# Moving columns of 256 read in turns from the two token blocks, with the weight ring at multiples of 64 bytes

## The reference

```python
z = einsum("bsd,dn->bsn", rmsnorm(x, g_mix), w_in)            # 1024 x 4608
# gated convolution branches, then
x = x + (g_a * (a @ w_a_out) + g_b * (s @ w_b_out)) @ w_o     # 512 x 1024 twice, 1024 x 1024
u = rmsnorm(x, g_ffn) @ w_up                                  # 1024 x 5632
x = x + (gelu(causal_conv(u_gate)) * u_value) @ w_down        # 2816 x 1024
x = x + sigmoid(rmsnorm(x) @ w_ple_gate) * (p @ w_ple)        # 1024 x 1024, 256 x 1024
# second block
proj = rms_norm(x) @ w_in_2                                   # 1024 x 2304, then two attentions
x = x + rms_norm(mix @ w_out_2)                               # 1024 x 1024
c = causal_conv(rms_norm(x) @ w_up_2)                         # 1024 x 8192
x = x + rms_norm((gelu(gate) * value) @ w_down_2)             # 4096 x 1024
```

## Time and profile before

| | us |
|---|---|
| median of 3 runs | 752.45 (752.36 to 752.64) |
| the profiled execution | 752.84 |
| its span, first to last instruction | 750.8 |
| TensorE matmul busy | 743.0 (99%) |
| VectorE busy | 578.7 (77%) |
| ScalarE busy | 452.0 (60%) |
| GpSimd busy | 210.6 (28%) |

### The profile page before, as it was taken

One profiled execution on the slowest core, in us unless ns is written; L12 is line 12 of the kernel. 1 busy time (PEld: TensorE's weight loads), 2 busy tenths in 40 slices (PEclk: granted clock), 3 DMA queues, 4 the chain that ended last, 5 costly groups with the idle time before them and its releaser, 6 DMA issues.

```text
span 750.8 us, 16764 instructions
## 1 busy us (share of the span) xinstructions
PE 743.0 (99%) x5950; PEld 722.7 (96%) x5950; DVE 578.7 (77%) x1049; ACT 452.0 (60%) x765; POOL 210.6 (28%) x136
## 2 busy tenths in 40 slices
PE   9999999999999999999999999999999999999997
PEld 9999999999999999999999999999999999988885
DVE  6899986877887887434987794799999999973333
ACT  7645456556665665445765798876766666643431
POOL 0477642460000000343464003322112212212220
PEclk9999999999999999999999999999999999999999
DMA  8566553565555567544444344365555555666551
GB/s 307 182 217 205 184 166 127 197 201 195 194 180 189 190 204 250 198 162 152 159 161 139 115 134 125 111 199 200 192 190 195 180 184 196 210 212 193 186 179 56
DMA packets 37917, 135.48 MB, mean 180 GB/s; under 512 B 4464, under 2 KB 4720, under 8 KB 37872
## 3 DMA queue, kind: packets, MB, share of 16 engines
q1 hardware_dynamic: 37728, 134.86, 54.4%
q10 hardware_dynamic: 144, 0.00, 0.0%
HBM read 133.80 MB, written 1.05 MB: 180 GB/s over the span
## 4 chain that ended last, share of the span: by engine, by line
PE 89%; DVE 3%; ACT 3%; issue 2%; POOL 1%; DMA 1%; SPq 0%; DVEq 0%; POOLq 0%; ACTq 0%
PE bank L1901 25%; PE bank L1902 25%; PE bank L1903 25%; PE bank L2349 4%; PE bank L2348 4%; PE bank L2347 4%; DVE w_lo L1223 1%; ACT w_hi L787 1%; DMA raw<-in_w_in 1%; POOL X L755 1%; PE bank L2176 1%; ACT score L1079 0%; PE bank L2200 0%; PE bank L1959 0%; DVE sumsq L1813 0%
## 5 line engine op out<-in xcount | busy, mean ns | idle before, releaser
L1901 PE MATMUL bank<-h_hi,w_hi 128*128 128x256 f32 x1372 | 385.9, 281 | 0.3 <-DVE w_lo L1223 0.2
L1902 PE MATMUL bank<-h_lo,w_hi 128*128 128x256 f32 x1372 | 382.9, 279 | 0.0
L1903 PE MATMUL bank<-h_hi,w_lo 128*128 128x256 f32 x1372 | 382.8, 279 | 0.0
L787 ACT ACTIVATE w_hi<-raw 128x1024 fp32r<-128x1024 f32 (+2 forms) x243 | 258.9, 1068 | 93.2 <-PE bank L1903 41.3
L1223 DVE TENSOR_TENSOR w_lo<-raw,w_hi 128x1024 fp32r<-128x1024 f32 (+2 forms) x187 | 236.6, 1268 | 85.9 <-ACT w_hi L787 84.0
L1901 PEld LDWEIGHTS bank<-h_hi,w_hi 128*128 128x128 f32 x1372 | 257.9, 188 | 1.8 <-DVE w_lo L1223 0.7
L1902 PEld LDWEIGHTS bank<-h_lo,w_hi 128*128 128x128 f32 x1372 | 258.0, 188 | 0.0
L1903 PEld LDWEIGHTS bank<-h_hi,w_lo 128*128 128x128 f32 x1372 | 257.9, 188 | 0.0
L636 POOL TENSOR_TENSOR w_lo<-raw,w_hi 128x1024 fp32r<-128x1024 f32 (+1 forms) x56 | 139.0, 2485 | 382.9 <-ACT w_hi L787 374.7
L1281 DVE TENSOR_TENSOR bank<-bank,scales 128x256 f32<-128x256 f32 x116 | 49.5, 430 | 26.3 <-PE bank L1903 17.6
L1572 DVE SCALAR_TENSOR_TENSOR cg<-bank,vec,cg 128x255 f32<-128x255 f32 x108 | 51.5, 476 | 0.7 <-ACT cg L1019 0.6
(11 more groups left out here) (235 smaller groups left out, 963.2 us busy)
## 6 DMA issues: line engine op xcount, KB each, us to landing
raw<-in_w_up SPq DMA_DIRECT2D x108, 512.0 KB, 3.3
raw<-in_w_in SPq DMA_DIRECT2D x53, 512.0 KB, 3.4
raw<-in_w_down SPq DMA_DIRECT2D x32, 512.0 KB, 4.2
raw<-in_w_down SPq DMA_DIRECT2D x16, 704.0 KB, 4.2
raw<-in_w_o SPq DMA_DIRECT2D x8, 512.0 KB, 4.3
raw<-in_w_gate SPq DMA_DIRECT2D x8, 512.0 KB, 3.4
raw<-in_w_out SPq DMA_DIRECT2D x8, 512.0 KB, 3.3
raw<-in_w_b_out SPq DMA_DIRECT2D x4, 512.0 KB, 3.6
```

Of the source, the lines that this page charges most:

```text
L787: nc.scalar.activation(hi_of(u)[:, cols], raw[s][:, cols], ACT.Copy).then_inc(hi_ready, 1)
L1901: nc.tensor.matmul(ps, wh, hi[:, k, :], start=start and n == 0, stop=False)
L1902: nc.tensor.matmul(ps, wh, lo[:, k, :], start=False, stop=False)
L1903: last = nc.tensor.matmul(ps, wl, hi[:, k, :], start=False, stop=stop and n == len(ks) - 1)
```

## The change

The moving columns and the PSUM columns of each 256-column product are put in another order: `in_turns` makes of the 256 columns the sequence tokens 0 to 3, 128 to 131, 4 to 7, 132 to 135, and so on. It is applied to the moving operand and to the output alike, so each token's sum lands in its old place. The access pattern of both operands gets three dimensions, of 32, 2 and 4 elements, with steps of 16, 512 and 4 bytes. The stationary operand, its weight load, the number of instructions, all waits and all DMAs stay.

`RING_PAST` becomes 0. The ring buffers then start 64 bytes past a multiple of 128, from byte 20,416 on, as the activations do. They end where they ended, so X and all that follows keep their addresses. `first_col` becomes 0 everywhere, so that the weights of "down2" from its fourth unit on keep their addresses as well. The first three units of "down2" move by 32 bytes.

```diff
-RING_PAST = 32
+RING_PAST = 0
...
+            def in_turns(columns):
+
+                return columns.rearrange("p (b i e) -> p i b e", b=2, e=4)
+
             def products(ps, s, block0, ks, hi, lo, start, stop, ready=None, w=None):
 
+                ps = in_turns(ps)
                 w_of = w or (w_hi[s], w_lo[s])
                 for n, k in enumerate(ks):
...
-                    nc.tensor.matmul(ps, wh, hi[:, k, :], start=start and n == 0, stop=False)
-                    nc.tensor.matmul(ps, wh, lo[:, k, :], start=False, stop=False)
-                    last = nc.tensor.matmul(ps, wl, hi[:, k, :], start=False,
+                    x_hi, x_lo = in_turns(hi[:, k, :]), in_turns(lo[:, k, :])
+                    nc.tensor.matmul(ps, wh, x_hi, start=start and n == 0, stop=False)
+                    nc.tensor.matmul(ps, wh, x_lo, start=False, stop=False)
+                    last = nc.tensor.matmul(ps, wl, x_hi, start=False,
                                             stop=stop and n == len(ks) - 1)
```

More of the change, by code:

```diff
@@ L1913, in lagging @@
                             wh, wl = (part[s][:, k * P:(k + 1) * P] for part in (w_hi, w_lo))
-                            nc.tensor.matmul(ps, wh, hi[:, k, :], start=start and k == ks[0], stop=False)
-                            nc.tensor.matmul(ps, wl, hi[:, k, :], start=False, stop=False)
+                            x_hi = in_turns(hi[:, k, :])
+                            nc.tensor.matmul(in_turns(ps), wh, x_hi, start=start and k == ks[0], stop=False)
+                            nc.tensor.matmul(in_turns(ps), wl, x_hi, start=False, stop=False)
                     if k != ks[0]:
@@ L1919, in lagging @@
                         for ps, s in tiles:
-                            last = nc.tensor.matmul(ps, w_hi[s][:, behind * P:(behind + 1) * P],
-                                                    lo[:, behind, :], start=False,
+                            last = nc.tensor.matmul(in_turns(ps), w_hi[s][:, behind * P:(behind + 1) * P],
+                                                    in_turns(lo[:, behind, :]), start=False,
                                                     stop=stop and k is None)
@@ L2012, in rounded_first @@
             def rounded_first(u):
-                ps = in_tile(u)
+                ps = in_turns(in_tile(u))
                 for k in range(DC):
                     wh = w_hi[slot(u)][:, k * P:(k + 1) * P]
-                    nc.tensor.matmul(ps, wh, h2_hi[:, k, :], start=k == 0, stop=False)
-                    nc.tensor.matmul(ps, wh, h2_lo[:, k, :], start=False, stop=False)
+                    nc.tensor.matmul(ps, wh, in_turns(h2_hi[:, k, :]), start=k == 0, stop=False)
+                    nc.tensor.matmul(ps, wh, in_turns(h2_lo[:, k, :]), start=False, stop=False)
                 unit_here(u)
                 for k in range(DC):
-                    last = nc.tensor.matmul(ps, w_lo[slot(u)][:, k * P:(k + 1) * P], h2_hi[:, k, :],
-                                            start=False, stop=k == DC - 1)
+                    last = nc.tensor.matmul(ps, w_lo[slot(u)][:, k * P:(k + 1) * P],
+                                            in_turns(h2_hi[:, k, :]), start=False, stop=k == DC - 1)
                 last.then_inc(unit_done, 1)
```

## The result

The changed kernel takes 802.8 us (median of 4 runs, 802.6 to 802.9) beside 752.4 us for the kernel before. The ratio is 1.067, with a 95% interval of 1.065 to 1.069. It is slower by 50 us, against a forecast of 724.5 us and a range up to 771.

What follows compares the result with a forecast made beforehand. TensorE's pitch of 116.7 ns was taken as the bound. A pitch of 110 saves 34.9 us, less waits of 2.5, 1.5, 1.3, 0.6 and 0.6: 28.4 off 752.84 gives 724.5 us, range 714 to 771.

Steps and rivals of the forecast that it cites:

- What bounds it: Whole kernel: TensorE's pitch of 116.7 ns; 5232 touched matmuls make each ns of pitch worth 5.2 us.
- The placement: Ring at the side buffers' remainder: alone, 120.0 against 116.7 ns on 5184 matmuls, +17 us.
- The turns: 256-column products: matmul and weight load keep a fixed distance, so pitch falls to 110 ns, saving 34.9 us.
- my streaming: Time of the moving columns alone: 0.417 ns a column, 106.7 ns for 256; the rest of a pitch is excess.
- The 110 ns of the transposes: Eight 128-column transposes with a weight load each take 0.88 us; taken as the pitch after the change.
- The unknown operand: Three-dimensional moving or PSUM operand: 0 to 0.417 ns at each of 64 jumps, at most 27 ns; taken as nothing.
- my own sign, over 125 ns in "up": A pitch over 125 ns in stage "up" was to mean rival 3.
- rival 3: 256-column products: each of 64 jumps, in SBUF or PSUM, costs one column step; 143.4 ns, +140 us, 892 us; chance 0.10.
- Rival 2: 256-column products: only where operands start matters, so turns do nothing; 120.0 ns, +17 us, 770 us; chance 0.20.
- Rival 1: 256-column products: weights load from the last column down, opposite to the matmul; 115.6 ns, 747 us; chance 0.12.
- rival 4: Whole kernel: placement costs what the turns give, 752.8 us within 1.5; chance 0.08.
- The 6.5 us for VectorE's limits: Saving lost to waits: "in" 2.5, "gate" 1.5, attention 1.3, joint before "up2" 0.6, "up2" 0.6 us.

Runs made afterwards that it cites:

- turns_only: The changed kernel with `RING_PAST = 32`, so the turns without the new placement: 801.8 us, 1.064 of the kernel before.
- narrow: Kernel before; in "up2" weight blocks of 128 or 72 columns: straight 117.4 and 118.7 ns, in turns of 4 126.8 and 129.5 ns.
- still: Kernel before; in "up2" one operand is one column reread: standing load 113.3 ns straight, 124.2 in turns; standing moving column 111.9 ns.
- far: Kernel before, turns of 4 elements from 4, 8, 16 and 32 blocks by ring slot: 133.8, 123.8, 115.3 and 117.8 ns.
- near: Kernel before; in "up2" runs of 32 bytes, 64 or 128 apart: 118.8, 118.0 ns; 64 bytes, 128 apart: 120.2; 8 bytes, 64 apart: 218.7.
- short_turns: The changed kernel with turns from 16 blocks instead of 2 (next read 64 bytes on) and the old ring placement: 743.8 us, 0.987 of before.
- short_turns_64: The changed kernel, its new ring placement kept, with turns from 16 blocks instead of 2: 748.1 us (742.0 to 751.5), 0.992 of before.
- moving_only: The changed kernel with moving columns read in turns but the output written straight in `products`: 807.6 us.

## Why the prediction was wrong

- **What bounds it: right.** Pitch times count is the whole kernel. 5232 touched matmuls at 5.2 us for each ns are 52 us for 10.0 ns, and the trace shows 51.
- **The placement: right.** 120.0 ns and +17 us, measured 120.0 and +14.7. The side buffers were a sound row for it. Between the two traces it is 13.7 us. The rest are waits, some 2.4 us less of them among the touched matmuls and 1 us among the others, which a slower TensorE covers.
- **The turns: the step that failed.** "If both go upward, they keep a fixed distance: after at most one stall at the start, nothing meets again." The pitch of `turns_only` was 126.7, not 110 ns. I had made one cause, two readers meeting, out of rows that showed only that an address matters and that, at equal remainders, an excess doesn't grow with the columns. At 32 bytes past it does: 116.7 ns with 256 columns and 233.3 with 512 are 10.0 and 20.0 ns over my streaming. That stood in the trace before, in the first three units of "down2", and I took the later ones. `narrow` shows that the excess doesn't follow the length of the weight load, and `still` that the load's walk makes up 3.6 ns of it and the moving reader's 5.0. The moving reader, whom I had taken as free, has a price of its own: 10.9 ns for the turns under a standing load. The 110 ns of the transposes was reached by no 256-column pattern; the lowest, with one column standing, was 111.9.
- **The unknown operand: the wrong end of the bound.** No row had a moving operand with jumps. I bounded it by 0 and 0.417 ns a jump and took 0, with the argument that four elements stay together. That term brought the 50 us: the turns alone took 801.8 us. The measured 10.0 ns is 0.16 ns for each of 64 jumps, between the bounds. They weren't bounds in general, though: short turns came out 1.4 ns below straight columns (`far`), and runs of two elements 0.80 ns a jump above (`near`). By my own sign, over 125 ns in "up", it is rival 3. That one had the kind of cause (the jumps cost) at 2.7 times its size, with each jump at one price and PSUM as guilty as SBUF, which the runs don't bear out, and at a chance of 0.10. With its 10 ns it would have given 752 + 52 = 804 us.
- **Rival 2** named the right sign and price for the placement, but the placement isn't what made the change slow: under the turns it makes no difference. **Rival 1** would need 115.6 ns, and **rival 4** 752.8 us.
- **Waits elsewhere.** The 6.5 us for VectorE's limits weren't put to the test in a slower kernel. In `short_turns` they were small: 1.9 ns less on 5232 matmuls are 10 us, and the span became 9 us shorter.
- **The range.** It left out rival 3 and ended at 771, so it had no place between a cost of 17 and one of 140 us. A term known only between two ends belongs in the range with the values between them, not as one rival at its far end.

## What to carry to other kernels

A matmul's pitch can depend on the order in which it reads its moving columns, at the same count, bytes and clock. Here it went from 115 to 219 ns at one placement by the pattern alone, while writing PSUM in runs of 16 bytes made no difference. A pattern that no row shows shouldn't be priced at nothing because a mechanism argues for it: its cost belongs in the forecast as a spread, and one run of that part alone, as `turns_only` here, settles it. A pattern with 16-byte runs 64 bytes apart is worth a try in a kernel of this kind, 1.3% here in `short_turns`, with its spread over several runs. Differences of up to 3 ns between single patterns should be read with care, since one pattern showed as much between its own rhythms.

## What the runs showed of the hardware

- Moving operand of 256 float32 columns, rounded form, runs of 16 bytes: 126.7 ns with 512 bytes to the next run, 133.8 with 256, 123.8 with 128, 115.3 with 64, 117.8 with 32, 116.7 straight. Two elements a run: 172.4 ns at 512 bytes, 218.7 at 64.
- PSUM written in runs of 16 bytes, 512 apart, with straight reads: no cost (120.0 ns with and without).
- Weights 64 bytes past a multiple of 128 like the activations, in place of 32: 120.0 against 116.7 ns with 256 moving columns, but 226.7 against 233.3 with 512.
- Cutting the weight block from 128 to 72 columns shortened the load from 0.19 to 0.14 us and the pitch by nothing.
- One and the same stream has several steady rhythms: 113.3 or 116.5 ns in `short_turns_64`, 126.7 or 130.0 in `moving_only`, 117.4 or 119.9 in `narrow`. What chooses between them is open.
